# Query weights loaded in halves, and three short VectorE copies written as sums, in the router of a two-layer transformer step

## The chip, the cores and the metric

The kernel is one program on one core of a Trainium2 chip. The metric is the device time of one execution in microseconds; the figure quoted is the median of several runs. The core has five engines that run their own instruction streams and meet on semaphores: TensorE (PE in the profile, its weight loads PEld), VectorE (DVE), ScalarE (ACT), GpSimd (POOL) and SyncE (SP, which here only issues transfers).

## The reference, cut to what matters

The model has two layers over 640 tokens of width 1024 (512 noisy latent tokens and 128 context tokens). A layer is a token mixer (attention in the first, pooling in the second) and then a PEER expert retrieval. The part that chooses the experts is called the router here:

```
q = (x @ wq).reshape(t, 8 heads, 2, 128)                # 1024 x 2048 weights per layer
sc = einsum('thpc,hpnc->thpn', q, keys)                 # 16 score rows of 128 per token
s_top, i_top = top_k(sc, 16)
cand = s_top[:, :, 0, :, None] + s_top[:, :, 1, None, :]
cs, ci = top_k(cand, 16)
i1 = take_along_axis(i_top[:, :, 0], ci // 16);  i2 = take_along_axis(i_top[:, :, 1], ci % 16)
idx = i1 * 128 + i2;  g = softmax(cs)
```

After it each token takes its 8 x 16 chosen rows of two tables of 16384 experts, weighs a GELU of the first by g and sums the second. All arithmetic is float32.

## The kernel before, in words

**Stages.** The program runs attention (to about 335 us of the profiled execution), the first router (345 to 652 us), the experts of layer one (to about 1724 us), pooling, the second router (1801 to 2077 us), the experts of layer two, and the last norm. In the experts stage three of the five token tiles are computed densely over all experts by TensorE, and the rows of the other two tiles are gathered by GpSimd and reduced by VectorE. The change touches the two routers only.

**A router's tiles and units.** The 640 tokens are 5 tiles of 128. The 2048 columns of `wq` are 4 chunks of 512 columns, 2048 KB each. For each tile TensorE multiplies the tile by the four chunks. Successive tiles walk through the chunks in opposite directions (`chunk_at`, line 161), and where two tiles meet on the same chunk it is loaded once, unless another load comes between. VectorE searches a tile in two halves (`search`, line 1233); half a tile is called a unit here, so a router has ten units, and a unit stands for two chunks of TensorE's work.

**The order written by hand.** `route_order` (line 176) is a list that TensorE and ScalarE both follow. A chunk is cut into four parts of two `k` blocks each (four matmuls are recorded for a block pair, line 1671). One unit `u` is eight places, r = 0 to 7: the parts 0 to 3 of one chunk, then those of the next. Behind parts 0 and 1 stand `turn` (transposes of the chunk before, line 1608) and `score` (line 1619). From unit 4 on `gates` (lines 1636 and 1637, sixteen small matmuls) stands at each place: it builds the dense gate matrix of eight tokens from one-hot rows. In the first router, units 4 to 8 end with an `ada` block (line 1686) and an `adat` block (line 1692, from the second on), which prepare modulation vectors of later layers from another 2048 KB weight chunk each. The second router has only two of these, at its very end.

**VectorE's side.** `search` finds the best 16 of each score row (`max`, `max_index`, `match_replace`), forms candidates (line 1305), copies the index row `topi` to float (line 1314, 128x64), finds the best 16 candidates, copies their places to 16 bits (line 1346, 128x64), builds two masks and copies the first index (line 1361, 128x4). Between these operations, one at every seventh, it writes the one-hot rows (`one_hots`, line 1420), eight per unit. The one-hot buffer `hot` has three slots, so the one-hot of a slot waits until TensorE has finished `gates` on the slot three back (line 1418). GpSimd multiplies the one-hot rows by the gates (line 703), and weighs and folds the masks (lines 669 to 693) on the same instruction stream; ScalarE copies PSUM banks out, scales one-hot rows (line 782) and every eight slots stores 4096 KB of gates to DRAM (line 802). The experts stage waits for the last of these stores.

**Loads.** SyncE issues all weight chunks of `wch` in one order (line 602). The buffer `wch` has two places of 2048 KB; chunk n goes into place n % 2. Before the load of chunk n SyncE waits until the last unit that reads chunk n-2 is done as a whole (line 609), and issues one transfer with one semaphore (line 615). TensorE waits for that semaphore ahead of part 0 of a chunk (`chunk`, line 1588). Loads of `ada` chunks take their turn in the same two places. In the first router the order from unit 4 on is: chunk X, chunk Y, `ada`, chunk X, chunk Y, `ada` and so on; so chunk X waits for chunk Y before it, and chunk Y waits for the `ada` chunk.

Of the kernel before, what the change touches and what calls it, by code (L numbers as in the profile page):

```python
# [18 lines left out]
ALU = mybir.AluOpType  # L19
# [9 lines left out]
K = D // P  # L29
DEPTH = 2  # L30
# [9 lines left out]
PH, NKEY, TOPK = 8, 128, 16  # L40
# [5 lines left out]
CH = 512  # L46
# [22 lines left out]
HALF = PH // 2  # L69
# [149 lines left out]
def build(nc, ins, outs):  # L219
# [20 lines left out]
    chunks = [(("ada",) + a, ("ada",) + a) for a in ADA_FIRST[:2]]  # L240
# [3 lines left out]
    LAST_LOAD, SHARED = {}, {}  # L244
# [17 lines left out]
    CN = {c[0]: n for n, c in enumerate(chunks)}  # L262
    for unit, first_use in SHARED.items():
        CN[unit] = CN[first_use]

    with ExitStack() as ctx:
        def sb(name, shape, dt=F32, where=None):
# [2 lines left out]
        def sem(name):  # L270
            return ctx.enter_context(nc.semaphore(name))

        bankA = [ctx.enter_context(nc.psum_tensor(f"bankA{i}", [P, 1024], F32)) for i in range(2)]
        bankD = [ctx.enter_context(nc.psum_tensor(f"bankD{i}", [P, 1024], F32)) for i in range(2)]
# [28 lines left out]
        with ExitStack() as front:  # L303
# [3 lines left out]
            wch = sb("wch", [P, 2, K * CH], where=front)  # L307
# [72 lines left out]
        qtok = std[:, 0:CH]  # L380
        high = std[:, CH:CH + P].bitcast(F16).rearrange("p (b t) -> p b t", b=2)
        low = aval[:, :].rearrange("p (b t) -> p b t", b=2)
        lowp = bankD[0][:, 768:768 + P]
        num16 = actg[:, :].bitcast(F16).rearrange("p (t j two) -> p t j two", j=2, two=2)
        early_buf = [qT[:, :, :].rearrange("p h t -> p (h t)")[:, i * K * CH:(i + 1) * K * CH] for i in range(len(EARLY))]
# [23 lines left out]
        att_in = sem("att_in")  # L409
        keys_ready = sem("keys_ready")  # L410
        pads_zeroed = sem("pads_zeroed")
        chunk_ready = [sem(f"chunk_ready{i}") for i in range(2)]
        early_ready = [sem(f"early_ready{i}") for i in range(len(EARLY))]
        adap_ready = [sem(f"adap_ready{i}") for i in range(len(ADA_POOL) - 1)]
# [131 lines left out]
        def _(sp):  # L546
# [53 lines left out]
                sp.sem_inc(stored[i], 16)  # L600
            sp.dma_start(small[:, :], small_d).then_inc(small_ready, 16)
            for n, (name, last) in enumerate(chunks):
                if n >= 2 and name != ("pool",):

                    u = chunks[n - 2][1]
                    if u in A:
                        sp.wait_ge(a_full, A[u] + 1)
                    elif u in R:
                        sp.wait_ge(r_full, R[u] + 1)
                    elif u in Mn:  # L610
                        sp.wait_ge(m_full, Mn[u] + 1)
                    else:
                        sp.wait_ge(d_full, Dn[u] + 1)
                src = source(name)
                sp.dma_start(wch[:, n % 2, 0:src.shape[1]], src).then_inc(chunk_ready[n % 2], 16)
                if n == 1:
                    sp.dma_start(const[:, :], const_d).then_inc(const_ready, 16)
                    for i in range(XCUT):
# [387 lines left out]
        def _(v):  # L1006
# [8 lines left out]
            def mark(ins):  # L1015

                steps[0] += 1
                ins.then_inc(step, 1)
                return steps[0]
# [208 lines left out]
            def routing(L):  # L1228
# [4 lines left out]
                def search(t, p):  # L1233
# [77 lines left out]
                    if s:  # L1311
                        v.wait_ge(mask_scaled, s)
                    v.wait_ge(step, found[7])
                    v.tensor_copy(topf[:, 1, :, :], topi[:, 1, :, :])
                    v.wait_ge(step, summed)
                    most, rest = [0] * HALF, [0] * HALF
                    for h in range(HALF):
# [25 lines left out]
                    if p:  # L1343
                        last.then_inc(gexp_in, 1)
                    v.wait_ge(step, chosen)
                    narrowed = mark(v.tensor_copy(ci, csi[:, :, :].rearrange("p t k -> p (t k)")))
                    if s:
                        v.wait_ge(mask_done, s)
                    v.wait_ge(step, narrowed)
# [8 lines left out]
                    if L and t >= DT:  # L1358
                        v.tensor_scalar(base, topi[:, 0, :, 0:1], float(L * NKEY), None, ALU.add)
                    else:  # L1360
                        v.tensor_copy(base, topi[:, 0, :, 0:1])
                    v.wait_ge(step, width)
                    within = mark(v.tensor_tensor(pick[:, 2, :], ci, pick[:, 1, :], ALU.bitwise_and))
                    v.tensor_tensor(topf[:, 0, :, 1:TOPK], topi[:, 0, :, 1:TOPK], topi[:, 0, :, 0:TOPK - 1], ALU.subtract)
# [76 lines left out]
                if L == 0:  # L1441
                    v.wait_ge(out_done, 32)
                v.memset(low4[:, :], TOPK - 1)
                for c, rows in enumerate((first_of, iota[:, 0:TOPK])):
                    v.tensor_copy(against[:, c, :].rearrange("p (a k) -> p a k", k=TOPK),
                                  rows.unsqueeze(2).to_broadcast([P, TOPK, TOPK]))
# [129 lines left out]
        def _(pe):  # L1576
            def chunk(name, cols=CH):

                if name[1:] in ADA_POOL[:-1]:
                    i = ADA_POOL.index(name[1:])  # L1580
                    pe.wait_ge(adap_ready[i], 16)
                    return adap[:, i, :].rearrange("p (k n) -> p k n", n=cols)
                if name in EARLY:
                    i = EARLY.index(name)
                    pe.wait_ge(early_ready[i], 16)
                    return early_buf[i].rearrange("p (k n) -> p k n", n=cols)
                n = CN[name]
                pe.wait_ge(chunk_ready[n % 2], 16 * (n // 2 + 1))
                return wch[:, n % 2, :].rearrange("p (k n) -> p k n", n=cols)
# [62 lines left out]
            def route(L):  # L1652

                for name in route_order(L):
# [5 lines left out]
                    if kind == "wq":  # L1660
# [3 lines left out]
                        if part == 0 and n >= 2:  # L1664
                            pe.wait_ge(r_free, n - 1)
                        if part == 0:
                            rows = chunk(whole)
                        for k in range(2 * part, 2 * part + 2):
                            if t == 0 and name[3] == 0:
                                pe.wait_ge(h_ready, (1 + 2 * L) * K + k + 1)  # L1670
                            last = pe.matmul(bank, hT[:, k, t * P:(t + 1) * P], rows[:, k, :], start=k == 0, stop=k == K - 1)  # L1671
                        if part == 3:
                            last.then_inc(r_full, 1)
                    elif kind == "turn":
# [354 lines left out]
```

## Time and profile before

| | us |
|---|---|
| median of 3 runs | 3171.96 (3168.54 to 3177.21) |
| the profiled execution, its own time | 3170.31 |
| its span, first to last instruction | 3167.9 |
| PE busy | 3001.9 (95%) |
| DVE busy | 2797.2 (88%) |
| POOL busy | 1892.7 (60%) |
| ACT busy | 1210.3 (38%) |

The mean granted clock of TensorE is 0.979 of full speed. In the page's 40 slices of 79 us, PE is busy nine tenths or more in nearly all slices of the experts stages; in the slices of the two routers DVE is the busier. Busy shares are means over stages with different limits, so the routers have to be read by themselves, with windows on the trace.

### The profile page before, as it was taken

What the parts mean: (1) busy time and instruction counts of PE and PEld (TensorE: products, weight loads), DVE (VectorE), ACT (ScalarE), POOL (GpSimd) and SP (SyncE); (2) the same over time, 40 slices, a digit from 0 to 9 for tenths busy, and PEclk for the clock granted to TensorE, in tenths of its full rate; (3) what the DMA queues carried; (4) which work ended last, traced back from release to release, by engine and by line L of the source; (5) the groups of instructions that cost most, each with busy time, mean ns of one, the idle gap of its engine ahead of it and who ended that gap; (6) DMA issues with size and microseconds to landing.
All of it is one profiled execution on the core that took longest, in us unless ns stands there. A gap on an engine that the chain in (4) does not pass through costs nothing.

```text
span 3167.9 us, 48593 instructions
## 1 busy us (share of the span) xinstructions
PE 3001.9 (95%) x15946; PEld 2501.8 (79%) x15946; DVE 2797.2 (88%) x5568; ACT 1210.3 (38%) x2077; POOL 1892.7 (60%) x1387
## 2 busy tenths in 40 slices
PE   7998987889999999999999898789999999999998
PEld 6856654479999999999997455579999999999997
DVE  3474597989999999999998689989999999999998
ACT  3332355633333333333333347633333333333333
POOL 1000166767677887776663058767777776777663
PEclk9999999999999999999999899999999999999999
DMA  5231366799999999999997446789999999999995
GB/s 238 72 133 49 136 237 266 295 378 409 408 407 409 403 407 385 410 409 401 409 398 269 185 171 266 304 333 406 409 410 399 409 401 387 409 395 410 408 402 223
DMA packets 248698, 1049.33 MB, mean 331 GB/s; under 512 B 23056, under 2 KB 72976, under 8 KB 205840
## 3 DMA queue, kind: packets, MB, share of 16 engines
q0 software_dynamic: 147456, 536.94, 43.0%
q1 hardware_dynamic: 99408, 460.72, 37.4%
q10 hardware_dynamic: 1728, 50.33, 3.7%
q8 instruction: 58, 0.95, 0.1%
q14 instruction: 48, 0.39, 0.0%
HBM read 994.68 MB, written 53.22 MB: 331 GB/s over the span
## 4 chain that ended last, share of the span: by engine, by line
PE 83%; DVE 11%; DMA 3%; issue 1%; ACT 1%; POOL 1%; DVEq 0%; SPq 0%; ACTq 0%
PE bankA L1713 11%; PE bankA L1711 11%; PE bankA L1712 11%; PE bankD L1724 7%; PE bankD L1725 7%; PE bankD L1723 7%; PE bankA L1671 4%; PE bankA L1725 4%; PE bankA L1724 4%; PE bankA L1723 4%; DVE hot L1420 2%; DMA wch<-in_wq 2%; PE bankD L1912 1%; PE bankD L1926 1%; PE bankA L1775 1%
## 5 line engine op out<-in xcount | busy, mean ns | idle before, releaser
L1711 PE MATMUL bankA<-hh,uh 128*128 128x384 f32 x2048 | 687.1, 335 | 1.7 <-DVE ul L1471 1.7
L1713 PE MATMUL bankA<-hh,ul 128*128 128x384 f32 x2048 | 687.4, 336 | 0.0
L1712 PE MATMUL bankA<-hl,uh 128*128 128x384 f32 x2048 | 685.9, 335 | 0.0
L709 POOL DMA_INDIRECT hT<-in_u,idxc x320 | 449.6, 1405 | 171.6 <-issue 76.1
L709 POOL DMA_INDIRECT hT<-in_v,idxc x320 | 440.7, 1377 | 182.2 <-issue 67.1
L857 ACT ACTIVATE wt<-bankA 128x384 f32<-128x384 f32 x256 | 126.0, 492 | 1046.3 <-PE bankA L1713 808.3
L1487 DVE SCALAR_TENSOR_TENSOR wch<-hT,a,wch 128x1024 f32<-128x1024 f32 x320 | 399.3, 1278 | 7.0 <-DMA hT<-in_v,idxc 5.2
L1724 PE MATMUL bankD<-vl,wh 128*128 128x512 f32 x1024 | 399.8, 390 | 0.0
L1725 PE MATMUL bankD<-vh,wl 128*128 128x512 f32 x1024 | 399.3, 390 | 0.0
L1723 PE MATMUL bankD<-vh,wh 128*128 128x512 f32 x1024 | 398.3, 389 | 0.0
L1478 DVE CUSTOM_DVE_ANT_0 hT<-hT,htok 128x1024 f32<-128x1024 f32 x320 | 383.1, 1221 | 15.6 <-DMA hT<-in_u,idxc 9.7
L1711 PEld LDWEIGHTS bankA<-hh,uh 128*128 128x128 f32 x2048 | 384.5, 188 | 13.0 <-issue 3.2
L1712 PEld LDWEIGHTS bankA<-hl,uh 128*128 128x128 f32 x2048 | 384.4, 188 | 9.8
L1713 PEld LDWEIGHTS bankA<-hh,ul 128*128 128x128 f32 x2048 | 384.2, 188 | 0.0
L669 POOL TENSOR_TENSOR mask<-mask,topf 128x1024 f16<-128x1024 f16 x36 | 69.2, 1929 | 490.3 <-DVE mask L1366 490.3
L1671 PE MATMUL bankA<-wch,hT 128*128 128x512 f32 x640 | 311.2, 618 | 25.0 <-DMA wch<-in_wq 23.7
L1499 DVE TENSOR_TENSOR vl<-vraw,vh 128x1024 fp32r<-128x1024 f32 x256 | 312.3, 1220 | 22.8 <-ACT vh L861 18.6
L709 POOL DMA_INDIRECT wch<-in_u,idxc x192 | 288.6, 1503 | 59.7 <-issue 59.7
L1471 DVE TENSOR_TENSOR ul<-uraw,uh 128x1024 fp32r<-128x1024 f32 x256 | 314.3, 1228 | 1.7 <-ACT uh L847 1.6
L709 POOL DMA_INDIRECT wch<-in_v,idxc x192 | 227.7, 1186 | 76.1 <-issue 54.7
L847 ACT CAST uh<-uraw 128x1024 fp32r<-128x1024 f32 x256 | 268.6, 1050 | 0.0
L861 ACT CAST vh<-vraw 128x1024 fp32r<-128x1024 f32 x256 | 266.7, 1042 | 0.0
(255 smaller groups left out, 5618.5 us busy)
## 6 DMA issues: line engine op xcount, KB each, us to landing
uraw<-in_uT SPq DMA_DIRECT2D x128, 1024.0 KB
vraw<-in_vP SPq DMA_DIRECT2D x128, 1024.0 KB
wch<-in_wq SPq DMA_DIRECT2D x34, 2048.0 KB, 8.4
gates_scratch<-gbuf ACTq DMA_DIRECT2D x12, 4096.0 KB, 14.1
wch<-gates_scratch SPq DMA_DIRECT2D x64, 768.0 KB
wch<-in_ada SPq DMA_DIRECT2D x19, 2048.0 KB, 8.7
wch<-in_qkv SPq DMA_DIRECT2D x3, 2048.0 KB, 23.6
adap<-in_ada SPq DMA_DIRECT2D x3, 2048.0 KB, 15.8
```

The source lines that it names most:

```text
L709: pool.indirect_dma_start(out=row_buf[slot], out_offset=None, in_=table.rearrange("l e d -> (l e) d"), in_offset=bass.IndirectOffsetOnAxis ...
L1471: v.tensor_tensor(ul[:, c, :], uraw[:, b, c * D:(c + 1) * D], uh[:, c, :].bitcast(F32), ALU.subtract).then_inc(ul_ready, 1)
L1478: v.tensor_tensor_reduce(out=row_buf[r % RING], in0=row_buf[r % RING], in1=htok[:, r % GT, :], scale=1.0, scalar=0.0, op0=ALU.mult, op1=AL ...
L1487: v.scalar_tensor_tensor(out=acc[:, r % GT, :], in0=row_buf[r % RING], scalar=a8[:, r:r + 1], in1=acc[:, r % GT, :], op0=ALU.mult, op1=ALU ...
L1499: v.tensor_tensor(vl[:, c % 2, :], vraw[:, b, c % 2 * D:(c % 2 + 1) * D], vh[:, c % 2, :].bitcast(F32), ALU.subtract).then_inc(vl_ready, 1)
L1671: last = pe.matmul(bank, hT[:, k, t * P:(t + 1) * P], rows[:, k, :], start=k == 0, stop=k == K - 1)
L1711: pe.matmul(abank[c], hi, hh[:, k, :], start=k == 0, stop=False)
L1712: pe.matmul(abank[c], hi, hl[:, k, :], start=False, stop=False)
L1713: last = pe.matmul(abank[c], lo, hh[:, k, :], start=False, stop=k == K - 1)
L1723: pe.matmul(y, hi, vh[:, c, a:a + 512], start=first, stop=False)
L1724: pe.matmul(y, hi, vl[:, c, a:a + 512], start=False, stop=False)
L1725: last = pe.matmul(y, lo, vh[:, c, a:a + 512], start=False, stop=final)
```

## The change: what it does

1. `wq` chunks are loaded by two transfers of 1024 KB, one for `k` = 0 to 3 and one for `k` = 4 to 7. Where chunk n-2 is also a `wq` chunk, the first half is issued when part 1 of the last unit on chunk n-2 is done (a new semaphore `q_half`, counted up at every part 1), and the second half when that unit is done, as the whole chunk was before. Where chunk n-2 is another chunk (an `ada` chunk, or attention's or the pooling's), both halves are issued after the old wait, one behind the other. TensorE waits for the first half ahead of part 0 and for the second ahead of part 2.
2. The three copies of VectorE (lines 1314, 1346 and 1361) become sums of the same source with zeros. The zeros are a 128x64 float32 row in PSUM (`zeros`, in the part of `bankD[0]` in which other small constants of the router stand), set once per router. The branch of line 1359 (the last two tiles of the second layer) is a `tensor_scalar` and stays as it is.

```diff
+    QUERY = [c[0] for c in chunks if c[0][0] == "wq"]
+    HALVES = {}
+    for name in QUERY:
+        b = CN[name] % 2
+        HALVES[name] = 1 + sum(CN[other] % 2 == b for other in QUERY[:QUERY.index(name)])
+    for unit, first_use in SHARED.items():
+        HALVES[unit] = HALVES[first_use]
+    SECOND = {}
+    for L in range(DEPTH):
+        for unit in route_order(L):
+            if unit[0] == "wq" and unit[4] == 1:
+                SECOND[unit[0:4]] = len(SECOND) + 1
...
+        zeros = bankD[0][:, 896:896 + HALF * TOPK]
...
             for n, (name, last) in enumerate(chunks):
+                if name[0] == "wq" and chunks[n - 2][0][0] == "wq":
+                    sp.wait_ge(q_half, SECOND[chunks[n - 2][1]])
+                    sp.dma_start(wch[:, n % 2, 0:K * CH // 2], source(name)[:, 0:K * CH // 2]).then_inc(half_ready[n % 2], 16)
                 if n >= 2 and name != ("pool",):
...
-                sp.dma_start(wch[:, n % 2, 0:src.shape[1]], src).then_inc(chunk_ready[n % 2], 16)
+                if name[0] == "wq":
+                    if chunks[n - 2][0][0] != "wq":
+                        sp.dma_start(wch[:, n % 2, 0:K * CH // 2], src[:, 0:K * CH // 2]).then_inc(half_ready[n % 2], 16)
+                    sp.dma_start(wch[:, n % 2, K * CH // 2:K * CH], src[:, K * CH // 2:K * CH]).then_inc(chunk_ready[n % 2], 16)
+                else:
+                    sp.dma_start(wch[:, n % 2, 0:src.shape[1]], src).then_inc(chunk_ready[n % 2], 16)
...
-                    v.tensor_copy(topf[:, 1, :, :], topi[:, 1, :, :])
+                    v.tensor_tensor(topf[:, 1, :, :], topi[:, 1, :, :], heads(zeros), ALU.add)
...
-                    narrowed = mark(v.tensor_copy(ci, csi[:, :, :].rearrange("p t k -> p (t k)")))
+                    narrowed = mark(v.tensor_tensor(ci, csi[:, :, :].rearrange("p t k -> p (t k)"), zeros, ALU.add))
...
-                        v.tensor_copy(base, topi[:, 0, :, 0:1])
+                        v.tensor_tensor(base, topi[:, 0, :, 0:1], heads(zeros)[:, :, 0:1], ALU.add)
...
+                v.memset(zeros, 0.0)
...
                         if part == 0:
-                            rows = chunk(whole)
+                            b = CN[whole] % 2
+                            pe.wait_ge(half_ready[b], 16 * HALVES[whole])
+                            rows = wch[:, b, :].rearrange("p (k n) -> p k n", n=CH)
+                        if part == 2:
+                            pe.wait_ge(chunk_ready[b], 16 * (CN[whole] // 2 + 1))
...
+                        if part == 1:
+                            last.then_inc(q_half, 1)
```

## Rows read from the trace of the kernel before

**Rows 1.** The page, section 4: engines' shares of the chain that ended last.
```profile
PE 83%; DVE 11%; DMA 3%; issue 1%; ACT 1%; POOL 1%; DVEq 0%; SPq 0%; ACTq 0%
```
**Rows 2.** Windows: stretch, busy us (and instructions) by engine, granted clock, DMA share, GB/s.
```profile
500.00:536.00 36.00, 28.90 (x205) 17.51 (x203) 28.47 (x127) 21.76 (x57) 23.16 (x16) 0.91 0.68 267
1892.00:1921.00 29.00, 24.84 (x185) 15.45 (x184) 28.90 (x131) 21.29 (x56) 23.43 (x16) 1.00 0.65 259
```
**Rows 3.** Waits, 400 to 2080 us and 440 to 660: total us, times, longest.
```profile
DVE hot L1420 <- PE bankD L1637: 29.0, 4, 8.6
PE bankA L1671 <- DMA wch<-in_wq: 22.0, 4, 6.7
```
**Rows 4.** Line 1671, idle time before it: total us, times; first router, then second.
```profile
  DMA wch<-in_wq: 23.1, 5
  DMA wch<-in_wq: 0.6, 2
```
**Rows 5.** Timeline of PE around two stalls: start, us, engine, line, [idle before].
```profile
453.09 2.81 PE L1671 MATMUL bankA<-wch,hT 128*128 128x512 f32 x4
463.86 1.92 PE L1686 MATMUL bankA<-wch,cs 128*32 128x512 f32 x16
470.22 3.75 PE L1671 MATMUL bankA<-wch,hT 128*128 128x512 f32 x4 [4.44 <-DMA wch<-in_wq]
538.59 1.05 PE L1692 MATMUL bankA<-const,adar 128*128 128x2 f32 x8
546.30 3.75 PE L1671 MATMUL bankA<-wch,hT 128*128 128x512 f32 x4 [6.66 <-DMA wch<-in_wq]
```
**Rows 6.** Timeline of SyncE's queue, the load in the first stall.
```profile
462.16 0.33 SPq L615 DMA_DIRECT2D wch<-in_wq  x1
```
**Rows 7.** Timeline of DVE, the one-hot behind the first stall.
```profile
476.40 1.22 DVE L1420 TENSOR_TENSOR hot<-actg,bankD 128x2048 f16<-128x2048 f16 x1 [5.88 <-PE bankD L1637]
```
**Rows 8.** Timelines of PE and DVE, one unit of the second router.
```profile
1919.28 1.94 PE L1671 MATMUL bankA<-wch,hT 128*128 128x512 f32 x4
...
1922.65 0.22 PE L1637 MATMUL bankD<-parts,hot 128*128 128x128 f16 x1
...
1926.26 1.94 PE L1671 MATMUL bankA<-wch,hT 128*128 128x512 f32 x4
...
1925.94 1.21 DVE L1420 TENSOR_TENSOR hot<-actg,bankD 128x2048 f16<-128x2048 f16 x1
```
**Rows 9.** Line 1314 in each router: ns min/median/max, first and last start, forms.
```profile
L1314 DVE CAST topf<-topi x10: 184/1550/1562, 371.9 to 634.0; 128x64 f32<-128x64 uint32 x10
...
L1314 DVE CAST topf<-topi x10: 185/1549/1557, 1827.9 to 2060.1; 128x64 f32<-128x64 uint32 x10
```
**Rows 10.** Timelines of POOL and DVE, one slow copy of line 1314.
```profile
1920.54 2.22 POOL L703 TENSOR_TENSOR parts<-hot,std 128x1024 f16<-128x1024 f16 x1 [0.37 <-DVE hot L1420]
...
1921.26 1.56 DVE L1314 CAST topf<-topi 128x64 f32<-128x64 uint32 x1
```
**Rows 11.** Lines 1341 and 1346, as in rows 9.
```profile
L1341 DVE TENSOR_TENSOR gt<-csv,bankD x20: 192/200/206, 375.5 to 2063.7; 128x64 f32<-128x64 f32 x20
...
L1346 DVE CAST ci<-csi x20: 184/192/197, 375.6 to 2063.8; 128x64 uint16<-128x64 uint32 x20
```
**Rows 12.** Landing times, 300 to 700 us: chunks of 2048 KB, then stores of 4096.
```profile
DMA to landing us min/median/max: 7.8/9.5/12.8
...
DMA to landing us min/median/max: 13.3/17.4/18.4
```
**Rows 13.** Windows, as in rows 2, during the second stall.
```profile
498.00:509.00 11.00, 4.07 (x41) 2.47 (x42) 8.74 (x40) 4.67 (x13) 7.25 (x4) 0.87 0.97 413
```
**Rows 14.** The chain that ended last, the end of the first router: start, us, what.
```profile
609.49 12.35 DMA wch<-in_ada
...
629.55 18.30 DMA gates_scratch<-gbuf
```
**Rows 15.** Timeline of PE, the first matmul of the second experts stage.
```profile
2077.33 0.41 PE L1711 MATMUL bankA<-hh,uh 128*128 128x384 f32 x1 [1.69 <-DVE ul L1471]
```

More of the change, by code:

```diff
@@ L264, in build @@
         CN[unit] = CN[first_use]
+    QUERY = [c[0] for c in chunks if c[0][0] == "wq"]
+    USE = {c[0]: c[1] for c in chunks}
+    HALVES = {}
[9 more added lines that the diff above has]
+                SECOND[unit[0:4]] = len(SECOND) + 1
     with ExitStack() as ctx:
@@ L411, in build @@
         pads_zeroed = sem("pads_zeroed")
+        half_ready = [sem(f"half_ready{i}") for i in range(2)]
+        q_half = sem("q_half")
         chunk_ready = [sem(f"chunk_ready{i}") for i in range(2)]
```

## The prediction, made blind

> **What bounds the kernel now.** I read the shares of the chain that ended last first. PE holds 83% and DMA 3% [rows 1]: the experts stages are PE's and the change does not touch them, so the whole question is how much earlier each router ends. Then I set windows of one unit in each router side by side. In the second router DVE is busy 28.90 of 29 us and PE 24.84: DVE is the bound there. In the first router a unit takes 36 us, DVE is busy only 28.47 of them, and PE's granted clock has fallen from 1.00 to 0.91 [rows 2]. So DVE does the same work in both and loses some 7 us per unit in the first. The waits say for whom: the one-hots of line 1420 wait 29.0 us in 4 places for PE's gates matmuls, and PE in turn waits 22.0 us in 4 places for a `wq` chunk [rows 3].
>
> The timeline shows one such place. PE ends its chunk Y, runs the `ada` block (463.86, 1.92 us), then waits 4.44 us for chunk X. The next four matmuls take 3.75 us where other groups of four take 1.94: the engine was idle before, and these run at 1.2 instead of 2.4 GHz. In the third place the wait is 6.66 us [rows 5, 8]. The load had been issued at 462.16, when chunk Y was done [rows 6]: chunk X has only the `ada` block to hide under. DVE stands still for 5.88 us at the one-hot that follows [rows 7].
>
> **Edit 1, the halves.** The four stalled chunks all have chunk Y, a `wq` chunk, two back, so all four get the early first half. What would be its timing in the first place? Part 1 of Y ends at 453.09 + 2.81 = 455.9. How long 1024 KB take no row shows alone. A whole chunk lands after 7.8 us at best and 12.8 at worst, a store of twice the size after 13.3 at best [rows 12]. The second 2048 KB of the store thus cost 5.5 us, 1024 KB 2.75, and a half lands after 7.8 - 2.75 = 5.1 us, or, scaled by 12.8 / 7.8 for a crowded queue, 8.4. Bounds: 2.75 and 12.8. I take 8.4, since the gates store is under way at that point. The half lands at 455.9 + 8.4 = 464.3; PE wants it at 463.86 + 1.92 = 465.8. It is hidden with 1.5 us to spare; at 12.8 it would be 2.9 us late, against 4.44 now. The second half is issued at 462.16 as before, and cannot land later than the whole did, 470.1. PE wants it at part 2, which comes 1926.26 - 1919.28 = 7.0 us after part 0 [rows 8], at 472.8. Hidden too. The wait goes, and with it the slow group (3.75 - 1.94 = 1.8 us).
>
> What is late next is the `ada` block itself. In an undisturbed unit of the second router the gates that free the slot are done at 1922.65 + 0.22 = 1922.9 and the one-hot starts at 1925.94: 3.1 us of slack [rows 8]. In the first place PE's extra time is 1.92 + 4.44 + 1.8 = 8.2, without what turn and the transposes behind it add, and DVE lost 5.88: a slack of 2.3 or more, which fits. Block and `adat` cost 1.92 + 1.0 = 2.9 us [rows 5], just inside. But edit 2 takes 1.36 us out of DVE's path just ahead of this one-hot, so the slack becomes 1.7. DVE will wait about 0.2 us in the first place (no `adat` there) and 1.2 in the other three: 3.8 in all. At both ends: 0 if PE runs ahead as before, 6 if the store delays it.
>
> Gain in the first router: 29.0 - 3.8 = 25.2 us. A fifth wait of PE, 23.1 - 22.0 = 1.1 us, lies before the stretch in which DVE is always busy and goes as well [rows 3, 4]. In the second router PE's waits are 0.6 us in all [rows 4], and go. Together 26.9. The price is 34 more transfers on SyncE's queue (0.33 us each to issue [rows 6]; it has nothing else to do), and nothing is queued behind a `q_half` wait that was issued sooner before: the `ada` load in front of it is issued two parts earlier. The two extra waits and the count at part 1 on PE carry no work; I put them at 0, between -0.5 and +2 us over 40 chunks.
>
> **Edit 2, the sums.** Line 1314 takes 1550 ns in the median and 184 ns at best, in either router [rows 9]. Six of ten are slow, the units with one-hots. In the slow case shown POOL runs from 1920.54 to 1922.76 and the copy ends at 1922.82 [rows 10]: it waits for POOL to finish. A sum of the same size with one input in PSUM exists, line 1341: 192 to 206 ns, and among its 20 there is no slow one; line 1346, still a copy, takes 192 and never hits a busy POOL [rows 11]. So the sum costs 0.20, the saving is 1.55 - 0.20 = 1.35, say 1.36 with the tail of the lock, for each slow copy. For the others, 0.01 us more each, 44 of them: 0.4 us, and I neglect it. Bounds of one slow copy: 0 (the sum waits as well) to 1.37.
>
> In the Trainium skill, "SBUF — State Buffer", section "Who interferes with whom", a copy may take the port pair that VectorE and GpSimd share and then one blocks the other fully, while an instruction with one SBUF input outside those modes does not contend. By it the saving is the full 1.35; if instead every `tensor_tensor` contended, it would be 0. The trace agrees with the first as far as it goes, in the 1.56 us of the copy and in the absence of a slow row of line 1341.
>
> All six count in the second router, since the last store of gates and the last search both follow DVE: 6 x 1.36 = 8.2 us. There PE's first expert matmul waits for DVE [rows 15]. In the first router the last one does not count. The end there hangs on the `ada` load issued at 609.49, when the last `wq` chunk is done, and on the store issued at 629.55 [rows 14]; the sixth slow copy comes behind that point. So 5 x 1.36 = 6.8 us.
>
> **Sum.** First router 25.2 + 1.1 + 6.8 = 33.1. Second 0.6 + 8.2 = 8.8. Together 41.9 us. From the profiled execution's own time, 3170.31 (span 3167.9 and 2.4 around it), that gives 3128.4. This execution lies 1.65 us below the median of the runs shown, so I forecast 3130.
>
> **The rivals.**
>
> *The queue becomes the bound.* With the stalls gone a unit of the first router moves 3 x 2048 + 4096 KB = 10.5 MB in 27.6 us (29 less the copy), 380 GB/s. In the second stall the engines moved 413 GB/s at a share of 0.97 [rows 13], so there is less than a tenth of room. If the halves come 2.9 us late as at the bound above, in four places, and bring part of the slow groups back, 10 to 12 us return: 3141. For it: a chunk lands after 9.5 us in the median and 12.8 at worst, so the engines are crowded there already [rows 12]. Against: the early issue spreads them.
>
> "SBUF — State Buffer" in the Trainium skill, section "Summary: rules for kernel authors", puts transfers from HBM at about 358 GB/s. By that 10.5 MB take 29.3 us, 1.7 us more than a unit, some 7 us in all (an estimate). The 413 GB/s measured here go past it, so the trace does not agree and I leave it in the range only.
>
> *The sums wait for POOL too.* Then edit 2 gives nothing (15.0 us less), but the slack at the `ada` blocks stays 3.0 and the 3.8 us of new waits fall away: 3130 + 15.0 - 3.8 = 3141. Against it stands line 1341; for it, that no row of line 1341 is seen to start while POOL runs.
>
> *The early halves don't come early.* If the first half lands no sooner than the second, for instance because transfers of one queue finish in order behind the `ada` load, only edit 2 is left: 3172 - 15.0 = 3157. Against: the `ada` load is issued two parts ahead, some 7 us [rows 8].
>
> *Slower.* Each transfer could hold the queue for nearly a whole chunk's time whatever its size, one after the other. At 7.8 us per half [rows 12] a unit of the first router needs 9.5 + 4 x 7.8 = 40.7 us of queue for its 27.6, and a unit of the second 31.2; in the first units of each router, where PE takes little more than 4 x 1.94 = 7.8 us per chunk, five loads each would stall PE by 7.8, less the 7.8 that each of the two chunks used twice gives back: 78 - 31 = 47. That is 4 x 13.1 + 5 x 3.6 + 47 = 117 us: 3247. It decides from a little over 6 us of queue per half, where the loss (at 6: 4 x 5.9 + 11 = 35) nears the gain. The 13.3 us of a store of 4096 KB speak against it: size counts, and 5.1 us is the estimate.
>
> "DMA: Bandwidth & Descriptors" in the Trainium skill, section "Anatomy of one DMA — SWDGE (gpsimd) path", gives about 2.0 us fixed per transfer, mostly the receipt at the end. Were this time of the queue, a half would hold it 4.4 us; no row here separates the two parts, and 4.4 is below the 6 from which it matters.
>
> **Chances.** Forecast 0.72, its own range 3123 to 3136. Queue bound 0.12, sums wait 0.06, halves not early 0.05, slower 0.03; 0.02 for no difference from what I have not seen. The range is 3121 to 3144: it takes in the forecast with 0 to 6 us of new waits, both cases at 3141, and a few us for the run-to-run spread of the median (3168.54 to 3177.21 here). A measurement of this kernel tells a change from none at about 0.3%, 10 us; so faster 0.94, same 0.02, slower 0.04.
>
> **What would show it.** Right: line 1671 waits for `wq` under 2 us in the first router, no group of four at 3.75 us behind an `ada` block, line 1420 waiting for PE under 6 us in all, units of the first router 28 to 30 us long, line 1314 at 0.20 us in all 20, the last store of the first router issued near 596, that of the second 42 us earlier than now. Wrong: a wait at part 2 for the second half, whole chunks landing later than 12.8 us, line 1314 above 1 us, or the `ada` load or the gates store at the end of the first router landing later than its 12.35 and 18.30 us.

## The result, and where the time went

| | us |
|---|---|
| median of 4 runs, changed kernel | 3152.8 (3147.35 to 3154.29) |
| median of 4 runs, kernel before, beside it | 3171.43 (3168.54 to 3177.21) |
| ratio | 0.9937 (0.9924 to 0.9951) |
| forecast | 3130, range 3121 to 3144 |
| the profiled execution, its own time | 3147.35 (span 3144.9) |

The change gains 18.6 us, not the 41.9 of the sum. The direction was right and the time came out above the range. The two profiled executions lie 22.96 us apart, and their PE timelines split that at the starts of the routers (first matmul group on a `wq` chunk) and at the `ul` operation ahead of the second experts stage:

| stretch | before, us | after, us | gained | forecast |
|---|---|---|---|---|
| start to first router | 345.30 | 343.62 | 1.7 | 0 |
| first router and the experts behind it | 1455.93 | 1442.11 | 13.8 | 33.1 |
| second router | 274.73 | 267.39 | 7.3 | 8.8 |
| the rest of the span | 1091.9 | 1091.8 | 0.1 | 0 |

So the second router nearly keeps its promise and the first lacks 19.3 us. The waits of the changed kernel from 440 to 660 us, as in [rows 3], name the place:

```profile
DVE hot L1444 <- PE bankD L1662: 25.8, 4, 7.1
PE bankA L1700 <- DMA wch<-in_wq: 13.4, 4, 4.0
```

PE waits 13.4 us for weights instead of 22.0, and VectorE's one-hots still wait 25.8 us for PE, where 29.0 stood before and 3.8 was forecast. Those 22.0 us too many are the missing gain, and a little more. The timelines of PE and VectorE, which answer to [rows 5, 7], show the stall at the same place, shorter, with a slow group of four still behind it (3.34 to 3.75 us in the four places):

```profile
463.88 3.34 PE L1700 MATMUL bankA<-wch,hT 128*128 128x512 f32 x4 [2.90 <-DMA wch<-in_wq]
499.35 3.75 PE L1700 MATMUL bankA<-wch,hT 128*128 128x512 f32 x4 [3.56 <-DMA wch<-in_wq]
...
468.91 1.22 DVE L1444 TENSOR_TENSOR hot<-actg,bankD 128x2048 f16<-128x2048 f16 x1 [4.55 <-PE bankD L1662]
505.07 1.22 DVE L1444 TENSOR_TENSOR hot<-actg,bankD 128x2048 f16<-128x2048 f16 x1 [7.14 <-PE bankD L1662]
```

What PE waits for is the early first half of chunk X. It is issued when it should be (449.47; the forecast's own point, part 1 of chunk Y done, moved with everything else). It does not land in time. The chain that ended last holds all four (start, us, what; two are shown, the other two took 15.65 and 15.44):

```profile
449.47 14.27 DMA wch<-in_wq
...
483.11 16.10 DMA wch<-in_wq
```

8.4 us was the forecast, 12.8 its bound. The queue of ScalarE shows what stands in the way: each of these halves is issued 2.5 to 3.2 us behind a store of gates of 4096 KB.

```profile
446.98 0.39 ACTq L826 DMA_DIRECT2D gates_scratch<-gbuf  x1
480.62 0.34 ACTq L826 DMA_DIRECT2D gates_scratch<-gbuf  x1
```

How the 16 transfer engines divide themselves stands in the queues' share in two stretches around the second of these (q10 is the store's queue, q1 SyncE's; packets, MB, share of the engines): 489 to 492 us, beside the store, and 498 to 501 us, behind it. What the profile counts as a packet is here one row of a tile.

```profile
q10 hardware_dynamic: 32, 1.05, 81.0%
q1 hardware_dynamic: 32, 0.26, 20.6%
...
q1 hardware_dynamic: 173, 1.28, 101.1%
```

In the first stretch each queue passes 32 packets (in the 3 us before it 30 and 22, in the 3 us behind it 31 and 32). They take turns, packet for packet, but a store's packet is 1.05 MB / 32 = 0.033 MB, a row of 32 KB, and a half's 0.26 / 32 = 0.008 MB, a row of 8 KB. The half moves at 0.26 MB in 3 us, 87 GB/s, while 437 GB/s pass in all. Both transfers consist of 128 packets, so the half is through when the store is. In the kernel before, chunk X was issued 10.4 us behind the store (451.80 and 462.16) and met only its end, and it had packets of 16 KB. The stretch of before in which the two are seen best side by side is 538 to 540 us, in the third place (the same columns):

```profile
q10 hardware_dynamic: 16, 0.52, 60.7%
q1 hardware_dynamic: 17, 0.28, 32.6%
```

Here too the packets are as good as equal in number, and the chunk gets half the store's bytes instead of a quarter.

Loading earlier moved the load into the store, and halving the transfer halved its packets: the same 128 rows, each half as long. Counted from the store, the first of the four is issued at 2.5 instead of 10.4 us, 7.9 sooner, and takes 14.3 instead of 7.9 us, 6.4 longer; PE's wait shrinks by the 1.5 us between, from 4.44 to 2.90.

In the Trainium skill, "DMA: Bandwidth & Descriptors", section "Queues, rings and completion order", each transfer engine serves the queues that have work in turn, and changes only at a packet's boundary. The 32 packets against 32 agree with it if one row is taken for a packet, and the shares by bytes follow from that; the page itself counts a packet as some 9 to 17 descriptors, and no run here shows how its packets and the profile's relate. The prediction did not weigh this rule.

### The profile page after: what moved, and what is told of

It is laid out like the page before. It is cut to its first block, busy times and chain, and to the rows that moved or that the text cites. A ratio compares the mean times of both kernels' runs of the same rounds, so it can differ in the third digit from the quotient of the medians.

```text
span 3144.9 us, 48631 instructions
## 1 busy us (share of the span) xinstructions
PE 2992.4 (95%) x15946; PEld 2497.5 (79%) x15946; DVE 2783.3 (89%) x5570; ACT 1209.5 (38%) x2077; POOL 1915.7 (61%) x1387
## 4 chain that ended last, share of the span: by engine, by line
PE 82%; DVE 12%; DMA 3%; issue 2%; ACT 1%; POOL 1%; SPq 0%; DVEq 0%; POOLq 0%; ACTq 0%
PE bankA L1742 11%; PE bankA L1744 11%; PE bankA L1743 11%; PE bankD L1755 7%; PE bankD L1756 7%; PE bankD L1754 7%; PE bankA L1756 4%; PE bankA L1700 4%; PE bankA L1755 4%; PE bankA L1754 4%; DVE hot L1444 3%; DMA wch<-in_wq 2%; PE bankD L1943 1%; PE bankD L1957 1%; PE bankA L1806 1%
## 5 line engine op out<-in xcount | busy, mean ns | idle before, releaser
L733 POOL DMA_INDIRECT hT<-in_u,idxc x320 | 457.1, 1428 | 167.0 <-issue 74.1
L733 POOL DMA_INDIRECT hT<-in_v,idxc x320 | 449.4, 1404 | 176.6 <-issue 68.0
L1700 PE MATMUL bankA<-wch,hT 128*128 128x512 f32 x640 | 308.2, 615 | 14.5 <-DMA wch<-in_wq 13.4
L887 ACT CAST wh<-wt 128x384 fp32r<-128x384 f32 x256 | 131.5, 514 | 357.7 <-DVE wt L1522 356.9
## 6 DMA issues: line engine op xcount, KB each, us to landing
adap<-in_ada SPq DMA_DIRECT2D x3, 2048.0 KB, 15.7
```

Source lines behind the costliest of these rows:

```text
L733: pool.indirect_dma_start(out=row_buf[slot], out_offset=None, in_=table.rearrange("l e d -> (l e) d"), in_offset=bass.IndirectOffsetOnAxis ...
```

## The experiments

The theory: the first half crosses a store and gets a fifth of the bytes, by the ratio of packet sizes, 1 to 4. The rivals: the transfer engines as a whole are the bound, whoever has which share (the forecast's first rival); the half is held up by the `ada` load that stands ahead of it in SyncE's own queue; or something else delays PE, and the 22 us have nothing to do with the stores. Medians are of several runs; the kernel before stood at 3171.14, 3171.53 and 3173.81 us in the three groups of runs, and each ratio is to it. Where a run gains is read from its profiled execution, from the first matmul group of a router on a `wq` chunk to the first matmul of the experts behind it. These lengths, in us, are of one execution each; outside the routers the executions differ by up to some 6 us.

| run | first router | second router |
|---|---|---|
| before | 313.30 | 276.10 |
| changed kernel | 299.83 | 268.76 |
| `e1_halves_only` | 302.29 | 274.76 |
| `e2_sums_only` | 312.67 | 269.62 |
| `e3_short_stores` | 279.51 | 268.74 |
| `e4_store_quarters` | 288.58 | 273.87 |
| `e7_last_whole` | 282.81 | 274.37 |
| `e10_store_in_two` | 284.85 | 270.00 |
| `e11_quarters_no_sums` | 285.74 | 282.07 |
| `e12_before_quarters` | 316.37 | 284.88 |

**The two edits alone.** `e1_halves_only` takes the sums back (one of the three is shown):

```diff
...
-                    v.tensor_tensor(topf[:, 1, :, :], topi[:, 1, :, :], heads(zeros), ALU.add)
+                    v.tensor_copy(topf[:, 1, :, :], topi[:, 1, :, :])
...
```

> Edit 1 alone; the three copies stay copies. Theory A (a first half creeps while a gates store is in flight, since the transfer engines take packets of the two queues in turn, 8 KB of a half against 32 KB of the store): the first halves still land 14 to 16 us after issue, PE still waits 3 to 4 us for each of four; the slack of 3.0 us at the one-hot is back, so DVE waits about 20 us for PE in the first router (29.0 before, 25.8 with both edits), and the time is some 10 us under the kernel before: 3161. Rival B (the two edits are independent, each worth half of the 20 us measured): DVE waits 25.8 as with both edits, 3166. The prediction's own sum for this edit: 3142.

3157.01 us, 0.9953 (0.994 to 0.9967). The four first halves land after 13.4 to 16.1 us. `e2_sums_only` is the other edit alone, with chunks loaded whole:

> Edit 2 alone; whole chunks are loaded as before. Theory A: line of the first sum at 0.20 us in all 20; in the second router the whole 8 us are gained less about 1.5 to 2 us by which a later sum waits longer for GpSimd's last subtraction; in the first router four of five savings only lengthen DVE's wait for PE (29.0 to about 34.4 us), so 1.4 us is left there. Together 8 us under the kernel before: 3163. Rival B: DVE's waits stay 29.0, the first router gains 6.8: 3157. The prediction's own sum: 3157.

3165.17 us, 0.9977 (0.9965 to 0.9989). The same wait in e1 and in e2, 440 to 660 us:

```profile
DVE hot L1443 <- PE bankD L1660: 19.4, 4, 6.4
```
```profile
DVE hot L1421 <- PE bankD L1639: 36.4, 4, 10.4
```

The halves alone give 14 us, the sums alone 6, together 18.6. With the sums the one-hots wait 6 to 7 us longer (19.4 to 25.8; 29.0 to 36.4): what VectorE saves in the first router, it mostly waits at the next one-hot. Of the sums' 15.0 us, e2 gains 6.5 in the second router, where DVE is the bound, and 0.6 in the first.

**Less of a store in the way.** `e3_short_stores` keeps everything of the change and shortens the stores, so that the gates are no longer those of the reference (the load of the gates, which changes too, is not shown):

```diff
...
-                act.dma_start(gates_d[2 * t + half], gbuf[:, half, :, :]).then_inc(stored[half], 16)
+                rows = P if t == DT - 1 else P // 4
+                act.dma_start(gates_d[2 * t + half, 0:rows], gbuf[0:rows, half, :, :]).then_inc(stored[half], 16)
```

> Both edits; every store of gates but the last of each router writes 32 of 128 partitions (1024 KB in packets of the old size), and the experts stage reads the gates of the last store for all tokens. Left out: three quarters of five of six stores, so the gates are not those of the reference. Theory A and also rival C (all bytes crowd the transfer engines alike): first halves land within 7 us, no wait of PE for wq above 1 us, DVE waits under 6 us for PE in the first router, some 20 us under the changed kernel: 3133. Rival D (the first half is held up by the ada load ahead of it on its own queue): halves land after 12 us or more as before, DVE waits over 20 us, 3150.

The edit shortens four of the six stores of a router, not five: both stores of the last tile stay at 4096 KB. The four early halves all meet a short one. 3130.13 us, 0.9872 (0.9857 to 0.9887): the forecast's time, though of a kernel that stores less. The early halves (line 621) land after 8.3 to 9.0 us, where the forecast took 8.4; first halves of chunk Y, issued when the short store has landed, after 5.2, where it worked out 5.1. The line's answer in the changed kernel, then that of lines 621 and 636 (the first half of a chunk Y, behind the `ada` block) in e3, then the one-hots' wait in e3:

```profile
L621 SPq DMA_DIRECT2D wch<-in_wq x4: 327/328/328, 449.5 to 554.2; - x4
DMA to landing us min/median/max: 14.3/15.5/16.1
```
```profile
L621 SPq DMA_DIRECT2D wch<-in_wq x4: 327/328/328, 452.3 to 540.9; - x4
DMA to landing us min/median/max: 8.3/8.6/9.0
...
L636 SPq DMA_DIRECT2D wch<-in_wq x4: 327/328/328, 463.9 to 552.7; - x4
DMA to landing us min/median/max: 5.1/5.2/5.4
```
```profile
DVE hot L1445 <- PE bankD L1663: 3.6, 4, 1.3
```

The 3.6 us stand against the forecast's 3.8, and the first router is 33.8 us shorter than before, against 33.1. The stores are the cause of the missing time. But e3 takes bytes away as well as a neighbour with long packets, so it does not yet part theory from first rival.

**The same bytes in smaller packets.** `e4_store_quarters` stores all the bytes, in four transfers of 8 KB packets (the counts that wait for them are not shown):

```diff
...
-                act.dma_start(gates_d[2 * t + half], gbuf[:, half, :, :]).then_inc(stored[half], 16)
+                for j in range(4):
+                    some = slice(j * NKEY // 4, (j + 1) * NKEY // 4)
+                    act.dma_start(gates_d[2 * t + half, :, some, :], gbuf[:, half, some, :]).then_inc(stored[half], 16)
```

> Both edits; each store of gates is issued as four transfers of 32 keys, so its packets are 8 KB like those of a half; the bytes are the same and the output is the reference's. Theory A: a half now gets half of the engines' bandwidth beside a store; first halves land after 8 to 10 us, PE's waits for wq fall from 13.4 to under 3 us in the first router, DVE's waits for PE to under 8 us, and the time to about 3135. Rival C (bytes alone crowd the engines, so packet size is nothing): landing 14 to 16 us, 3152. Rival D as well: 3152.

3150.7 us, 0.9939 (0.9925 to 0.9952). The time was missed by 16 us, the mechanism was not. Its time is that of the changed kernel. The queues of e4 from 487 to 490 us, its first halves, and the waits:

```profile
q10 hardware_dynamic: 109, 0.76, 60.4%
q1 hardware_dynamic: 64, 0.52, 41.3%
```
```profile
L621 SPq DMA_DIRECT2D wch<-in_wq x4: 327/328/328, 451.3 to 543.0; - x4
DMA to landing us min/median/max: 9.4/10.2/10.9
```
```profile
DVE hot L1446 <- PE bankD L1664: 6.6, 5, 1.8
PE bankA L1646 <- issue: 8.6, 5, 3.9
```

With the bytes unchanged the half gets 0.52 MB in 3 us instead of 0.26, lands 5 us sooner, no wait for `wq` is left and the one-hots wait 6.6 us instead of 25.8. The transfer engines are as busy as in the changed kernel (both shares together 101.7%, there 101.6%) and only divided otherwise, so the first rival falls. The 109 packets of the store's queue are not 64, and 16 of them are under 512 B. From 547 to 550 us, in the fourth place, the turns are even:

```profile
q1 hardware_dynamic: 78, 0.64, 50.4%
q10 hardware_dynamic: 78, 0.62, 49.0%
```

What takes the gain back is new. Four issues hold ScalarE for up to 4.47 us, and the last store of a router, which the experts wait for, has landed 22.63 and 21.18 us behind the last of its four issues, where the whole store of the changed kernel took 18.2 and 17.2: beside its 4.19 MB, SyncE's expert weights now take 3.59 MB of the second router's last store (2019 to 2041 us), where the changed kernel's store let 2.29 MB pass (2025 to 2043). From the chain of e4 and the timeline of its ScalarE queue:

```profile
600.32 22.63 DMA gates_scratch<-gbuf
...
2019.33 21.18 DMA gates_scratch<-gbuf
```
```profile
448.77 4.47 ACTq L828 DMA_DIRECT2D gates_scratch<-gbuf  x4
```

`e7_last_whole` leaves the last store of each router in one piece (`q = 1 if t == DT - 1 and half else 4`):

> Both edits; stores as four transfers of 32 keys as in e4, but the last store of each router is one transfer as before. In e4 the stalls went (DVE waited 6.6 us for PE) and the end stores took 22.6 and 21.2 us. Theory E (e4's gain was lost at the routers' ends): with the last store whole they take 18.3 and 14.7 again, and the time falls by some 8 to 10 us against e4, to 3141. Rival F (it was lost to the four issues on ScalarE in each unit): no more than 3 us better than e4, 3148.

3139.8 us, 0.9904 (0.9888 to 0.992), as expected; the last stores land after 18.3 and 18.48 us. By the traces the gain on e4 lies in the first router (5.8 us); the second is no shorter (274.37 against 273.87 us), and the cause of that stays open. With long packets a store is fast where the end waits for it, and with short ones it lets others pass.

**The store moved, not cut.** `e6_late_stores` issues every store but the last four places later:

```diff
+LATE = 4
...
-                if g % (NSLOT // 2) == NSLOT // 2 - 1:
+                h = g - LATE if g < ALL_SLOTS - 1 else g
+                if h >= 0 and h % (NSLOT // 2) == NSLOT // 2 - 1:
...
```

> Both edits; every store of gates but the last of each router is issued four places (half a unit) later on ScalarE, just behind the issue of chunk X's second half. Same transfers, same packets, same bytes. Theory A (a first half creeps only while a store is in flight): first halves land within 7 us, PE's waits for wq fall from 13.4 to under 1 us, DVE's waits for PE in the first router to under 6, the stores at the routers' ends take 18 us as before, and the time is some 20 us under the changed kernel: 3132. Rival C (the bytes of a unit crowd the engines however they are placed): DVE's waits stay over 15 us, 3148 or more. A late store could also hold up the next use of its half of the buffer; then ScalarE waits at the gates copies, and 3140.

3149.48 us, 0.992 (0.9905 to 0.9935): missed by 17 us. The stall only went to the next load. The answers for line 623 (first halves of chunk X, now clear of the store) and line 638 (first halves of chunk Y, issued 2 us behind it, for three of which PE now waits), and PE's waits:

```profile
L623 SPq DMA_DIRECT2D wch<-in_wq x4: 328/328/328, 452.8 to 550.6; - x4
DMA to landing us min/median/max: 5.2/5.4/5.7
...
L638 SPq DMA_DIRECT2D wch<-in_wq x4: 328/328/328, 464.4 to 559.6; - x4
DMA to landing us min/median/max: 14.2/16.1/16.6
```
```profile
PE bankA L1719 <- DMA wch<-in_ada: 14.1, 3, 8.8
PE bankA L1702 <- DMA wch<-in_wq: 10.0, 3, 3.8
```

This is the cleanest pair for the cause. Both lines load 1024 KB in 8 KB packets; beside the store they take 14.2 to 16.6 us, away from it 5.2 to 5.7 (and line 636 of e3, which has a second half close behind it as line 638 has, 5.1 to 5.4). It also answers the rival of SyncE's own queue: the `ada` load stands 6.8 us ahead of the first of the early halves in both kernels (442.71 and 449.47 us, here 446.07 and 452.83), and here the half lands after 5.7 us. My expectation had treated the other loads as patient, and they were not. `e8_late_ada_halves` gives the `ada` chunks of e6 their first half early too (`QUERY` takes in the `ada` chunks two behind a `wq` chunk):

> As e6, and an ada chunk whose predecessor in the same place is a wq chunk is loaded in halves in the same way. At the end of the first router PE waits 4 to 8 us for such a chunk while gates are still to come, and the last store hangs on it. Theory A with this: the wait goes, since the first half is issued two parts sooner; the last store is issued some 4 us sooner, 3128. Rival: the end is held by the load of the next ada chunk or by VectorE instead, 3132 as e6.

3146.31 us, 0.9923 (0.9909 to 0.9937): missed by 18. PE waits 19.4 us for `ada` instead of 14.1, but not for the early halves: no wait for one is in the trace. It waits for the last two `ada` chunks, which are still loaded whole (line 641); they are issued 1.9 and 7.9 us behind a store and land after 19.6 and 27.1 us. `e5_before_late` is the late store in the kernel before:

> The kernel before, with the late stores of e6 and nothing else. Theory A: whole chunks X no longer meet a store in its first part, they land after about 8 instead of 7.9 to 11.9 us, so PE's waits fall from 22.0 to some 14 to 16 us and the time by 6 to 8 us, to 3164. Rival C: no change, 3171.

3189.35 us, 1.0049 (1.0036 to 1.0063): slower, against the expected sign. Chunk X is now issued beside the store and lands after 12.62 to 14.10 us, where it had 7.9 to 11.9; waits of e5 as in [rows 3]:

```profile
DVE hot L1422 <- PE bankD L1639: 42.0, 4, 11.4
PE bankA L1673 <- DMA wch<-in_wq: 34.3, 4, 9.7
```

The place of the store in the kernel before was the better one for its loads: chunk X met only its end. The change moved the load and left the store.

**How much of it is packets.** `e12_before_quarters` cuts the stores of the kernel before as in e7:

> The kernel before, whole chunks and copies, with the stores of e7. Theory A: chunk X, issued while a store is in flight, lands after 8 to 9 us instead of up to 11.9, since its 16 KB packets now outweigh the store's 8 KB; PE's waits for wq fall from 22 to some 16 us, the time to 3165: the packets alone don't replace the early half. Rival: the same 3171.

3182.06 us, 1.0039 (1.0025 to 1.0053): missed, slower. Chunk X lands after 7.99 to 10.89 us, hardly sooner, since it met the end of the store only; PE still waits 22.8 us in 4 places. What is left is a price, which goes by its places and times with the four issues: in the first router ScalarE stands 8.8 us and PE 8.4 us behind them, in the second PE 17.9 us in 6 places, and the second router is 8.8 us longer. The short packets are worth something only together with the early halves.

`e10_store_in_two` looks for the balance: two transfers of 16 KB packets, the last store whole (`q = 1 if t == DT - 1 and half else 2`).

> As e7, but stores in two transfers (packets of 16 KB), the last whole. Theory A by shares: against 8 KB packets of a half the store takes two thirds of the engines instead of a half (and four fifths with 32 KB); first halves land after 11 to 13 us, PE waits 1 to 2 us for each, DVE's waits for PE 10 to 15 us, 3145. If two issues on ScalarE cost much less than four (e7: ScalarE stands 4.5 us over the first four), part of that comes back. Rival C (bytes alone): as e7, 3140, with landings of 9.6 us.

3137.04 us, 0.9886 (0.9871 to 0.9901), the fastest version that stores everything; its interval overlaps that of e7, so which of the two is better is open. By the traces it gives up 2.0 us of e7's gain in the first router and wins 4.4 back in the second. Its queues from 487 to 490 and from 460 to 463 us, its first halves, its waits, and its two waits of PE with the group behind each:

```profile
q10 hardware_dynamic: 55, 0.90, 70.2%
q1 hardware_dynamic: 45, 0.37, 29.1%
...
q10 hardware_dynamic: 53, 0.85, 67.2%
q1 hardware_dynamic: 53, 0.43, 34.2%
```
```profile
L621 SPq DMA_DIRECT2D wch<-in_wq x4: 327/328/328, 452.6 to 545.6; - x4
DMA to landing us min/median/max: 12.1/12.5/13.0
```
```profile
DVE hot L1447 <- PE bankD L1665: 8.0, 4, 4.0
PE bankA L1703 <- DMA wch<-in_wq: 2.7, 2, 1.6
```
```profile
465.80 1.96 PE L1703 MATMUL bankA<-wch,hT 128*128 128x512 f32 x4 [1.65 <-DMA wch<-in_wq]
...
526.11 3.36 PE L1703 MATMUL bankA<-wch,hT 128*128 128x512 f32 x4 [1.08 <-DMA wch<-in_wq]
```

Landings were as expected; waits of 8.0 us were less than the 10 to 15 expected, and the time was 8 us under the expected 3145. The two issues cost ScalarE 0.82 to 0.87 us in the first router and up to 3.25 in the second. After a wait of 1.65 us the group still runs in 1.96 us, after one of 1.08 us in 3.36: the length of the wait alone does not decide whether a slow group follows, and what does was not tried.

The three kernels give one rough formula. A half's 1.05 MB at the rate its queue had beside the store (0.26, 0.37 and 0.52 MB in 3 us) take 12.1, 8.5 and 6.1 us, and the landings have medians of 15.5, 12.5 and 10.2: some 4 us more than the bytes. With the stretches of even turns (0.43 and 0.64 MB) the last two become 7.3 and 4.9 us, and what comes on top is 3 to 5 us.

**Two checks on the rest.** `e11_quarters_no_sums` is e7 with the copies of the kernel before:

> e7 with the three copies as before. Theory A: with the stalls gone the slow copies are on the path in both routers; the time is 8 to 12 us above e7, 3150, of it some 6 in the second router, and DVE waits under 3 us for PE in the first. Rival H (the copies hide under the ada blocks in the first router even without stalls): only the second router's 6 us, 3146.

3150.56 us, 0.9931 (0.9918 to 0.9945), as expected in all: with the stalls gone the sums are worth 10.8 us (3139.8 against 3150.56), with them 4.2 (3152.8 against 3157.01, intervals that overlap). But by the traces the difference is not made in the first router: there the sums give 2.9 us without the stalls and 2.5 with them, in the second router 7.7 and 6.0. `e9_quarters_ada` adds early `ada` halves to e7:

> e7 (both edits, stores in four transfers but the last of each router) and ada chunks behind a wq chunk in halves too. Theory A: at the end of the first router PE no longer waits the two times (7.7 us in all in e7) for an ada chunk, the last store there is issued some 4 us sooner, 3136. Rival G: what the ada load gains, the next load or the store's landing gives back, 3140.

3142.91 us, 0.9901 (0.9886 to 0.9916): no better than e7. PE's wait for `ada` falls from 7.7 to 5.1 us, but the waits behind ScalarE's issues rise from 8.4 to 14.6 us and the one-hots' from 6.7 to 13.3.

## Why the prediction missed, step by step

- **What bounds it, and whose wait it is:** right. The second router gained by VectorE, the first by its waits.
- **When the first half can be issued:** right, at part 1 of Y (449.47 us here).
- **How long a half takes: the step that failed.** "I take 8.4, since the gates store is under way at that point", with 12.8 as the end; measured 14.3, 16.1, 15.7 and 15.4. The 5.1 us for a half alone were right (5.1 to 5.4 in e3). The scale of a "crowded queue", 12.8 / 7.8, was read from two whole `ada` chunks with 16 KB packets: the one of 7.8 us was issued 5.6 us ahead of a store (446.21 and 451.80), the one of 12.8 us 14 us behind one (613.95 and 599.90). The half meets nearly a whole store, with 8 KB packets. So 12.8 us was no bound either, and a multiple of a landing time does not carry over: the share of the engines has to be worked out for the pair. The row was there, though: the stretch of before shown above has 17 packets of SyncE's queue beside 16 of the store's, with their bytes.
- **"The wait goes, and with it the slow group":** wrong for that reason. PE waits 13.4 us in four places, 4.0 us at most, and the groups behind them still take 3.34 to 3.75 us.
- **New waits of 3.8 us at the one-hots, since the slack is 1.7:** right once the stall is gone (3.6 in four places in e3).
- **Edit 1's price, 34 more issues and two more waits, at nothing:** nothing in the runs speaks against it. e3 has all of them and reaches 3130.13.
- **Edit 2, 0.20 us for each sum whether POOL runs or not:** right, all 20 of line 1338; the 20 of line 1370 take at most 0.22 us and the 16 of line 1385 at most 0.16:

```profile
L1338 DVE TENSOR_TENSOR topf<-topi,bankD x20: 200/209/220, 369.9 to 2035.3; 128x64 f32<-128x64 uint32 x20
```

- **Its 8.2 us in the second router, and 0.6 of waits:** 7.3 measured for the 8.8. Counted from the router's start the last store of gates is issued 9.3 us sooner, but it lands after 17.2 us instead of 14.7: the prediction let it land as before. Beside it SyncE's queue moves 2.29 MB (2025 to 2042.5 us), where it moved 1.12 before (2050 to 2065 us). ScalarE's cast to `hh` waits for this store and POOL's `hl` subtraction for the cast. The `idx` operation behind the last search, which reads two inputs in SBUF, ended with `hl` in both kernels; it starts earlier now and takes longer, 4.59 us instead of 2.67. The cast before and after, then the timelines of VectorE and POOL after:

```profile
2064.82 2.75 ACT L836 CAST hh<-hT 128x3072 fp32r<-128x3072 f32 x1 [11.51 <-DMA gates_scratch<-gbuf]
...
2042.52 2.75 ACT L860 CAST hh<-hT 128x3072 fp32r<-128x3072 f32 x1 [14.00 <-DMA gates_scratch<-gbuf]
...
2047.61 4.59 DVE L1411 SCALAR_TENSOR_TENSOR idx<-i 128x128 uint32<-128x128 f32 x1
...
2045.35 6.70 POOL L763 TENSOR_TENSOR hl<-hT,hh 128x3072 fp32r<-128x3072 f32 x1 [11.31 <-ACT hh L860]
```

  The 1.9 us are a gain given back further down, since the lock ends with `hl` and `hl` hangs on the store: the median of the four rows of this `idx` line is 0.28 us. In the Trainium skill, "SBUF — State Buffer", section "Who interferes with whom", an instruction of VectorE with two SBUF inputs contends with a GpSimd instruction that reads SBUF, and the end at 2052.20 beside POOL's 2052.05 agrees.
- **Its 6.8 us in the first router:** a gross figure. The prediction's own 3.8 us of new waits come from the sums, so net it gave them 3.0 us there once the stalls are gone, and e7 against e11 shows 2.9. Ahead of the full stalls they give 0.6 (e2), of the shortened ones 2.5.
- **The rivals.** "The queue becomes the bound" came nearest in kind, late halves and slow groups, but named the wrong resource and was capped at 2.9 us per place. "The early halves don't come early" is what happened in the main: issued 7.9 us sooner, ready 1.5 sooner in the first place. It was priced as all or nothing. A case between, at 3150, was worth a chance: its mechanism, a half stretched to the end of the store, was on the table with the 13.3 to 18.4 us of a store in [rows 12].

In the sum: 25.2 us of stall became 3.2, and the second router lacks 1.5 us. If the other terms held, 41.9 - 22.0 - 1.5 = 18.4, and the profiled executions differ by 22.96, of which 1.7 lie ahead of the first router and 2.7 stay unexplained in the first.

## What to carry to other kernels

When a load is moved earlier, ask what is in the transfer engines at that moment: beside another queue it got its share here packet by packet, so by the ratio of packet sizes, and cutting a tile along the row makes its packets shorter and its share smaller. Price its landing from the bytes each queue passes side by side, not by scaling a landing time. Where a load must cross a store that nobody waits for, cut the store's packets down, not the load's, and count what the extra issues cost where nothing is to be gained (the second router lost 5.6 us with four of them); where somebody waits for the store, keep it whole; and where an engine's time is saved ahead of a stall, expect little of it (0.6 of 6.8 us in e2).

## What the runs showed of the hardware that was not expected

- Two queues took turns packet for packet, 32 to 32 in 3 us, with packets of 32 and 8 KB: 350 and 87 GB/s. With 16 against 8 KB, 53 to 53 packets gave shares of 67.2 and 34.2%; with four store transfers of 8 KB, 78 to 78 gave 49.0 and 50.4%. The turns are not always even: other stretches of these runs had 55 to 45 and, small ones included, 109 to 64.
- A store of 4096 KB in four transfers beside expert weights took 22.63 and 21.18 us behind its last issue, in one 17.2 to 18.5.
- Four issues in a row on ScalarE's queue took 1.87 to 4.65 us in e4, e7, e11 and e12, two 0.82 to 3.25 in e10, one 0.32 to 0.40. Why the times spread so was not tried.
